# One expert's rows kept in SBUF and added by a one-hot product; earlier loads of the others; picks of three tiles on VectorE and three shifts on GpSimd

## Chip, cores, metric

One core of a Trainium2 chip runs the whole program. The metric is device time in microseconds, the median of the runs. Engines: TensorE (PE; PEld is its weight load), VectorE (DVE), ScalarE (ACT), GpSimd (POOL) and SyncE (SP, which issues most DMAs).

## The reference, cut to what matters

One encoder layer on 1152 tokens of width 1024 (1024 of a prompt, 8 x 16 of samples): a token mixer, a cross attention, and a mixture of experts, each followed by a layer norm. What the change touches is the last third:

```python
def hier_moe(x, lp):          # top-1 of 4 groups, then top-2 of 8 experts in it
    ...
    gate = (softmax(top_v) * pg[:, None]).reshape(-1)     # two gates per token
    ...
    h = silu(xb @ w_g[e]) * (xb @ w_u[e])                 # 128 rows of one expert
    return (h @ w_d[e]) * wts[:, None]
    ...
    out = zeros_like(xt).at[buf_tok].add(yb)              # two expert rows per token

x = layer_norm(ALPHA * x + hier_moe(x, lp), lp['ln3_g'], lp['ln3_b'])
```

## The kernel before

All is float32. Tokens are nine tiles of 128 rows (eight of the prompt, one of samples). The large products use two rounded parts of each operand (`high` and `low`, of type float32r) and three matmuls; products of plain float32 take two passes of TensorE for 512 columns.

*Experts.* A block is one expert with up to 128 gathered rows; there are 32 blocks (`NE`) and none more with these inputs, since no expert has over 128 rows. For block b, SyncE loads the weights (gate and up in two halves, L652, and down, L663) as VectorE frees the areas (semaphores `gu_low`, `down_low`); ScalarE rounds them (L1634, L1644), VectorE takes the remainders (`take_low`, L1747); GpSimd gathers the rows (L2357) two blocks ahead; TensorE turns them (L1292) and multiplies (L1245). The results of block b are copied from PSUM to `yo[b % 2]` by ScalarE (L1675; for the last block, in two halves, L1698 and L1700), and GpSimd scatters them to `expert_rows` in DRAM (L2364), one row for each pick: row 2 x token + k for pick k. Unused slots carry an index out of bounds and are dropped. `ye_out[u]` counts the scatters from `yo[u]`, which is also what ScalarE waits for before it fills the buffer again.

*Tail.* SyncE loads the nine tiles of x (`xl`, L689) and the layer norm's gain and shift, when the last block's gate and up products are through. Then it waits for both scatters' semaphores and loads, for each tile, the two expert rows of each token (`yk`, 1 MB a tile, L695). The weighted sum x + gate0 y0 + gate1 y1 is done for two tiles by VectorE (L2203, L2204), and for seven by TensorE: four plain float32 products with diagonal matrices of the gates (`diag`, made by VectorE in L2191; L1348) into `T[0]` or `T[1]`, which VectorE adds to x (L2199), with the row sum as a by-product. Buffers alternate, so a product waits for the sum two before it.

*Layer norm of a tile*, with p the place of the tile in the order `SEQ`: VectorE sum (`sum_rows`), its mean; ScalarE square with row sum (L1724); VectorE adds epsilon (`add_eps`, L2217); GpSimd takes the inverse root (`inverse_deviation`, L2394), on which VectorE waits for the shift factor (`shift_of`, L2212); ScalarE normalises (L1729); GpSimd multiplies by the gain (`times_gain`, L2399, both operands in SBUF); VectorE adds the shift (`add_shift`, L2222, from a copy of it in PSUM). The last two tiles are done by VectorE alone (L2227, L2232). SyncE stores tile after tile (L698). The order on each engine is written by hand. VectorE's:

```python
sum_rows(0)
for p in range(PT):                       # PT = 8
    sum_rows(p + 1)
    if p > 0: shift_of(p - 1)             # waits for root p-1 of GpSimd
    if p > 2: add_shift(p - 3)
    add_eps(p)
```

GpSimd's is: root 0; then for p from 0 to 6 the root of p+1 and the gain of p, with root 8 ahead of the last gain.

Of the kernel before, what the change touches and what calls it, by code (L numbers as in the profile page):

```python
# [49 lines left out]
def encoder_layer_kernel(nc, A, O):  # L50
# [55 lines left out]
    ye_dram = nc.dram_tensor("expert_rows", [2 * NT * P, D], f32).ap()  # L106
    ye_pairs = ye_dram.rearrange("(r k) d -> r k d", k=2)

    ctx = ExitStack()
    with ctx:  # L110
# [212 lines left out]
        yk = [area(WA + (11 + 2 * t) * D, 2, D) for t in range(NT)]  # L323
        SEQ, BY_PE = (0, 2, 1, 3, 4, 5, 6, 7, 8), (1, 3, 4, 5, 6, 7, 8)
# [101 lines left out]
        def _(sp):  # L426
# [261 lines left out]
            for t in range(NT):  # L688
                sp.dma_start(xl[t], x2_dram[t * P:(t + 1) * P, :]).then_inc(ln_in, 16)  # L689
            sp.dma_start(gain3, A["ln3_g"].to_broadcast([P, D])).then_inc(ln_in, 16)  # L690
            sp.dma_start(shift3, A["ln3_b"].to_broadcast([P, D])).then_inc(ln_in, 16)
            sp.wait_ge(ye_out[1], 16 * (NE // 2))
            sp.wait_ge(ye_out[0], 16 * more + 16 * (NE // 2))
            for t in range(NT):
                sp.dma_start(yk[t], ye_pairs[t * P:(t + 1) * P, :, :]).then_inc(last_in[t], 16)  # L695
            for n, t in enumerate(SEQ):
                sp.wait_ge(y_ready, n + 1)
                sp.dma_start(tokens(y_p, y_s, t), xl[t]).then_inc(y_out, 16)  # L698
# [3 lines left out]
            sp.wait_ge(edge_out, 16 * (4 + NB))  # L702
# [6 lines left out]
        def _(pe):  # L709
# [631 lines left out]
            for n, t in enumerate(BY_PE):  # L1341
                pe.wait_ge(last_in[t], 16)
                if n > 1:
                    pe.wait_ge(sum_done, NORMS + SEQ.index(BY_PE[n - 2]) + 1)
                out = T[n % 2]
                for k in (0, 1):
                    for c in (0, 512):
                        got = nc.tensor.matmul(out[:, c:c + 512], diag[2 * n + k], yk[t][:, k, c:c + 512], start=(k == 0), stop=(k == 1))  # L1348
                got.then_inc(picks_ps, 1)

        @block.scalar
        def _(act):
# [318 lines left out]
            def results(b, u, uses):  # L1671
                if not (isinstance(uses, int) and uses == 0):
                    act.wait_ge(ye_out[u], 16 * uses)
                act.wait_ge(down_used, 4 * b + 4)
                nc.scalar.copy(yo[u], M[1][:, :]).then_inc(ye_rows, 1)  # L1675
# [20 lines left out]
            act.wait_ge(ye_out[1], 16 * ((NE - 1) // 2))  # L1696
# [3 lines left out]
            nc.scalar.copy(yo[1][:, 512:], M[0][:, 512:]).then_inc(ye_rows, 1)  # L1700
# [14 lines left out]
            act.wait_ge(ln_in, 48 + 16 * (NT + 2))  # L1715
            act.wait_ge(ye_rows, more + NE)
            nc.scalar.copy(M[1][:, :], shift3).then_inc(gates_ready, 1)
# [20 lines left out]
        def _(dve):  # L1738
# [359 lines left out]
            nc.vector.tensor_single_scalar(route_tok[:, 0:NE], route_out[:, 0:NE], 1, ALU.logical_shift_right).then_inc(routes_ready, 1)  # L2098

# [17 lines left out]
            nc.vector.tensor_tensor(gates[:, 1, :], gates[:, 0, :], r_e2, ALU.mult)  # L2117
# [40 lines left out]
            split_down(NE - 1, (3,))  # L2158

# [28 lines left out]
            then(nc.vector.tensor_scalar(gates, gates, 1.0 / ALPHA, None, ALU.mult))  # L2188
# [4 lines left out]
            dve.wait_ge(ln_in, 48 + 16 * (NT + 2))  # L2193

            def sum_rows(p):
                u, t = p % 2, SEQ[p]
                if t in BY_PE:
                    dve.wait_ge(picks_ps, BY_PE.index(t) + 1)
                    nc.vector.scalar_tensor_tensor(xl[t], xl[t], 1.0, T[BY_PE.index(t) % 2][:, :], ALU.mult, ALU.add,  # L2199
                                                   accum_out=moments[u][:, 0:1]).then_inc(sum_done, 1)  # L2200
                else:
                    dve.wait_ge(last_in[t], 16)
                    then(nc.vector.scalar_tensor_tensor(xl[t], yk[t][:, 0, :], gates[:, 0, t:t + 1], xl[t], ALU.mult, ALU.add))  # L2203
                    nc.vector.scalar_tensor_tensor(xl[t], yk[t][:, 1, :], gates[:, 1, t:t + 1], xl[t], ALU.mult, ALU.add,  # L2204
                                                   accum_out=moments[u][:, 0:1]).then_inc(sum_done, 1)
# [27 lines left out]

            sum_rows(0)
            for p in range(PT):
# [5 lines left out]
                if p > 2:  # L2241
                    add_shift(p - 3)
                add_eps(p)

# [10 lines left out]
        def _(pool):  # L2255
# [114 lines left out]
            for b in range(NE):  # L2370
                if b + 2 < NE:
                    pool.wait_ge(xgT_ps, b + 1)
                    gather(b + 2, b % 2)
                if b > 1:
# [12 lines left out]
            pool.wait_ge(ln_in, 48 + 16 * (NT + 2))  # L2387
# [52 lines left out]
```

## Time and profile before

| | us |
|---|---|
| runs, median (lowest, highest) | 1660.57 (1656.14, 1665.41) |
| the profiled execution | 1661.41 |
| its span, first to last instruction | 1659.6 |
| mean granted TensorE clock, share of full | 0.978 |

The page gives a row of busy shares in 40 slices of 41.5 us. TensorE is near 9 tenths nearly everywhere. The experts run from about 1030 to 1607 us, with DMA at 9 tenths and 380 to 396 GB/s; the tail is the last 53 us. An average over the span says little on the tail: it has to be read from the chain of waits (what released what, back from the last instruction) and from the timeline. Times in the rows are microseconds from the start of the span.

### The profile page before, as it was taken

To read this page: it belongs to the slowest core of one execution; us is meant where nothing else is said; L and a number is where in the kernel's file an instruction comes from. 1 tells how busy PE (TensorE), PEld (TensorE's weight loads), DVE (VectorE), ACT (ScalarE), POOL (GpSimd) and SP (SyncE) were. 2 spreads that over 40 slices of the span, in tenths; PEclk is the share of its full clock that TensorE was granted. 3 is DMA by queue.
4 is the path that set the end of the run, shared out by engine and by line. 5 is a ranking of instruction groups with operands and counts; after the bars stand their busy time and mean duration, and the time that the engine had idled before them with its cause. 6 is when DMAs were issued, how large, how long until landed. Compare 5 with 4: busy or idle time off the path is not lost.

```text
span 1659.6 us, 21156 instructions
## 1 busy us (share of the span) xinstructions
PE 1585.4 (96%) x8402; PEld 1306.9 (79%) x8402; DVE 993.6 (60%) x1315; ACT 762.7 (46%) x1089; POOL 254.2 (15%) x220
## 2 busy tenths in 40 slices
PE   7999999899998999999999988999999999999966
PEld 3578887788886788999877767888888888888852
DVE  1411111477756366122455447999999898998846
ACT  2311121334436102222422222878888788888734
POOL 0000000300017471000022111111111111111105
PEclk9999999999999999999999987999999999999987
DMA  9611111510021644300335545899999999999976
GB/s 352 225 60 46 67 61 58 200 59 20 10 65 52 224 157 178 115 26 14 119 123 173 182 170 193 314 386 384 385 390 396 388 393 388 392 396 384 377 266 288
DMA packets 84001, 351.66 MB, mean 212 GB/s; under 512 B 23346, under 2 KB 26034, under 8 KB 62020
## 3 DMA queue, kind: packets, MB, share of 16 engines
q1 hardware_dynamic: 73780, 330.43, 52.7%
q0 software_dynamic: 9216, 18.89, 3.0%
q8 instruction: 64, 1.05, 0.3%
q10 hardware_dynamic: 912, 1.05, 0.2%
q14 instruction: 29, 0.24, 0.0%
HBM read 321.93 MB, written 43.15 MB: 220 GB/s over the span
## 4 chain that ended last, share of the span: by engine, by line
PE 58%; DMA 20%; DVE 13%; ACT 5%; issue 1%; SPq 1%; POOL 0%; DVEq 0%; POOLq 0%; ACTq 0%
DMA beside<-in_w_exp_up 19%; PE M L974 12%; DVE rounded L1747 11%; PE T L780 6%; PE M L771 5%; PE T L714 4%; PE M L854 4%; PE M L714 2%; ACT rounded L1634 2%; PE T L1048 2%; PE T L1046 2%; PE T L1047 2%; PE M L738 2%; PE M L1080 2%; PE M L1062 2%; PE T L1348 2%
## 5 line engine op out<-in xcount | busy, mean ns | idle before, releaser
L1747 DVE TENSOR_TENSOR rounded<-beside,rounded 128x1024 fp32r<-128x1024 f32 (+1 forms) x397 | 471.7, 1233 | 100.0 <-ACT rounded L1634 47.9
L1245 PE MATMUL M<-rounded 128*128 128x512 f32 x1920 | 467.2, 394 | 4.7 <-issue 2.5
L1245 PEld LDWEIGHTS M<-rounded 128*128 128x128 f32 x1920 | 360.3, 189 | 80.7 <-issue 2.6
L1634 ACT CAST rounded<-beside 128x1024 fp32r<-128x1024 f32 x256 | 259.3, 1050 | 79.3 <-DMA beside<-in_w_exp_up 71.9
L974 PE MATMUL M<-rounded 128*128 128x512 f32 x864 | 209.9, 398 | 2.9 <-ACT rounded L1504 1.6
L974 PEld LDWEIGHTS M<-rounded 128*128 128x128 f32 x864 | 160.6, 190 | 36.3 <-issue 2.2
L1644 ACT CAST rounded<-beside 128x1024 fp32r<-128x1024 f32 x128 | 124.9, 1048 | 27.0 <-DMA beside<-in_w_exp_down 27.0
L1747 DVE TENSOR_TENSOR rounded<-T,rounded 128x512 fp32r<-128x512 f32 (+2 forms) x98 | 92.5, 948 | 32.4 <-ACT rounded L1517 17.7
L1245 PE MATMUL T<-rounded 128*128 128x512 f32 x384 | 108.7, 398 | 0.0
L2364 POOL DMA_INDIRECT expert_rows<-beside,route_out x32 | 38.6, 1205 | 409.7 <-ACT beside L1675 389.6
L714 PE MATMUL T<-tables,arena 128*128 128x128 f32 x572 | 79.7, 283 | 15.9 <-DMA arena<-in_mem_prompt 8.0
L714 PEld LDWEIGHTS T<-tables,arena 128*128 128x128 f32 x572 | 68.2, 145 | 32.4 <-issue 9.0
L1245 PEld LDWEIGHTS T<-rounded 128*128 128x128 f32 x384 | 70.0, 189 | 13.0
L1457 ACT ACTIVATE arena<-T,negmax 128x384 f32<-128x384 f32 (+3 forms) x64 | 47.4, 740 | 71.2 <-DVE negmax L1839 71.2
L854 PEld LDWEIGHTS M<-arena 128*128 128x128 f32 x576 | 72.0, 191 | 2.6 <-DVE arena L1857 0.2
L854 PE MATMUL M<-arena 128*128 128x64 f32 x576 | 71.7, 270 | 0.1
L1046 PE MATMUL T<-rounded 128*128 128x256 f32 x248 | 71.0, 286 | 0.0
L1048 PE MATMUL T<-rounded 128*128 128x256 f32 x248 | 70.2, 283 | 0.0
L1047 PE MATMUL T<-rounded 128*128 128x256 f32 x248 | 70.2, 283 | 0.0
L780 PE MATMUL T<-rounded,x_high 128*128 128x512 f32 x270 | 65.4, 394 | 0.0
L771 PE MATMUL M<-rounded,x_high 128*128 128x416 f32 (+1 forms) x270 | 61.2, 377 | 1.4 <-ACT x_high L1368 1.1
L1899 DVE SCALAR_TENSOR_TENSOR arena<-arena,M 128x1024 f32<-128x1024 f32 x18 | 22.0, 1220 | 63.6 <-PE M L974 63.6
(339 smaller groups left out, 2345.5 us busy)
## 6 DMA issues: line engine op xcount, KB each, us to landing
beside<-in_w_exp_gate SPq DMA_DIRECT2D x64, 1024.0 KB, 7.5
beside<-in_w_exp_up SPq DMA_DIRECT2D x64, 1024.0 KB, 10.3
beside<-in_w_exp_down SPq DMA_DIRECT2D x32, 2048.0 KB, 11.7
arena<-x_rows SPq DMA_DIRECT2D x27, 512.0 KB, 4.6
x_rows<-arena SPq DMA_DIRECT2D x18, 512.0 KB, 3.0
arena<-expert_rows SPq DMA_DIRECT2D x9, 1024.0 KB, 12.7
arena<-in_x_prompt SPq DMA_DIRECT2D x16, 512.0 KB, 3.9
arena<-in_cache_mem_k SPq DMA_DIRECT2D x8, 1024.0 KB, 5.7
```

Source lines behind the costliest of these rows:

```text
L714: got = nc.tensor.transpose(out[:, k * P:(k + 1) * P] if width == P else out[0:width, k * P:(k + 1) * P], rows[:, k * width:(k + 1) * widt ...
L771: got = nc.tensor.matmul(M[u][:, at:at + c1 - c0], x[:, k * P:(k + 1) * P], part[k][:, c0:c1], start=(k == 0 and part is w_in_high and x i ...
L780: got = nc.tensor.matmul(T[u][:, c:c + CW], x[:, k * P:(k + 1) * P], part[k][:, GC + c:GC + c + CW], start=(k == 0 and part is w_in_high a ...
L854: got = nc.tensor.matmul(o, prT[n % 2][:, c, :], value[:, c, h * DV:(h + 1) * DV], start=(c == 0), stop=(c == i))
L974: got = nc.tensor.matmul(out[:, c:c + 512], x[k], part(k)[:, c:c + 512], start=(k == 0 and x is hi and part is high), stop=(k == KT - 1 an ...
L1046: nc.tensor.matmul(out, high(k)[:, d * P:(d + 1) * P], x1T[:, 0, k], start=(k == 0), stop=False)
L1047: nc.tensor.matmul(out, high(k)[:, d * P:(d + 1) * P], x1T[:, 1, k], start=False, stop=False)
L1048: got = nc.tensor.matmul(out, low(k)[:, d * P:(d + 1) * P], x1T[:, 0, k], start=False, stop=(k == KT - 1))
L1245: got = nc.tensor.matmul(out, x[xs], (high, low)[ws](w)[:, c:c + 512], start=(first and n == 0), stop=(last and n == 2))
L1634: nc.scalar.copy(as_both(high(c)), both_raw(c)).then_inc(gu_high, 1)
L1644: nc.scalar.copy(high(8 + c), down_raw[:, c, :]).then_inc(down_high, 1)
L1747: return nc.vector.tensor_tensor(out, x, highs.bitcast(f32), ALU.subtract)
```

## The change

Three things. (1) The results of the last block don't go to DRAM. ScalarE scales them by the gates of their picks while it copies them to `yo[1]` (`own_gate`, fetched with an indirect gather from the new DRAM tensor `gates_by_pick`, which SyncE writes from `gate_rows`). They are rounded and split (`y_hi`, `y_lo`), and TensorE adds them to every tile by a product with a one-hot matrix (`own_slot`, nine tiles made by VectorE from the slots' tokens). Their rows of `expert_rows` are zeroed at the start by a scatter of a cleared buffer. (2) The loads of the picked rows wait for the scatter of block 30, and for VectorE being done with the last weights, in whose areas seven of them now land. Gain and shift come behind the first two. (3) The tiles go in the order 0 to 8. VectorE does the picks of tiles 1, 4 and 7 (`sum_picks`), TensorE of the other six, and a sum of TensorE's buffer follows for all nine. GpSimd adds the shift to the first three tiles.

The diff, cut to its core:

```diff
-        SEQ, BY_PE = (0, 2, 1, 3, 4, 5, 6, 7, 8), (1, 3, 4, 5, 6, 7, 8)
+        SEQ, BY_PE = (0, 1, 2, 3, 4, 5, 6, 7, 8), (0, 2, 3, 5, 6, 8)
+        SHIFTED = 3
...
@@ SyncE, after the loads of block 1's gate and up
+                else:
+                    sp.wait_ge(kT_ready, 4 + 2 * H + 1)
+                    sp.dma_start(gates_dram.rearrange("(t p k) c -> p t (k c)", p=P, k=2), gate_rows).then_inc(edge_out, 16)
...
@@ SyncE, tail
             sp.wait_ge(gu_used, 8 * more + 8 * NE)
-            for t in range(NT):
+            for t in SEQ:
                 sp.dma_start(xl[t], x2_dram[t * P:(t + 1) * P, :]).then_inc(ln_in, 16)
-            sp.dma_start(gain3, A["ln3_g"].to_broadcast([P, D])).then_inc(ln_in, 16)
-            sp.dma_start(shift3, A["ln3_b"].to_broadcast([P, D])).then_inc(ln_in, 16)
-            sp.wait_ge(ye_out[1], 16 * (NE // 2))
+            sp.wait_ge(gu_low, 8 * more + 8 * NE)
+            sp.wait_ge(down_low, 4 * more + 4 * NE)
+            sp.wait_ge(ye_out[1], 16 + 16 * (NE // 2))
             sp.wait_ge(ye_out[0], 16 * more + 16 * (NE // 2))
-            for t in range(NT):
+            for t in SEQ:
                 sp.dma_start(yk[t], ye_pairs[t * P:(t + 1) * P, :, :]).then_inc(last_in[t], 16)
+                if t == SEQ[1]:
+                    sp.dma_start(gain3, A["ln3_g"].to_broadcast([P, D])).then_inc(mv_in, 16)
+                    sp.dma_start(shift3, A["ln3_b"].to_broadcast([P, D])).then_inc(mv_in, 16)
...
@@ TensorE, tail
+            for n, t in enumerate(SEQ):
                 if n > 1:
+                    pe.wait_ge(sum_done, NORMS + n - 1)
                 out = T[n % 2]
+                if t in BY_PE:
+                    pe.wait_ge(last_in[t], 16)
+                    for k in (0, 1):
+                        for c in (0, 512):
+                            nc.tensor.matmul(out[:, c:c + 512], diag[2 * BY_PE.index(t) + k], yk[t][:, k, c:c + 512], start=(k == 0), stop=False)
+                if n == 0:
+                    pe.wait_ge(att_high, 4 + 4 * H + 1)
+                    pe.wait_ge(kT_ready, 4 + 2 * H + 2)
+                for part in (y_hi, y_lo):
                     for c in (0, 512):
+                        got = nc.tensor.matmul(out[:, c:c + 512], own_slot[:, t * P:(t + 1) * P], part[:, c:c + 512],
+                                               start=(t not in BY_PE and part is y_hi), stop=(part is y_lo))
                 got.then_inc(picks_ps, 1)
...
@@ ScalarE, last results and tail
-            nc.scalar.copy(yo[1][:, 0:512], M[0][:, 0:512])
+            nc.scalar.activation(yo[1][:, 0:512], M[0][:, 0:512], ACT.Identity, scale=own_gate)
...
             act.wait_ge(ye_rows, more + NE)
+            nc.scalar.copy(y_hi, yo[1]).then_inc(att_high, 1)
+            act.wait_ge(mv_in, 16 * NB + 32)
             nc.scalar.copy(M[1][:, :], shift3).then_inc(gates_ready, 1)
...
@@ VectorE, before the experts; after the last splits; tail
+            then(nc.vector.tensor_scalar(gates, gates, 1.0 / ALPHA, None, ALU.mult))
+            nc.vector.tensor_copy(gate_rows, gates.rearrange("p k t -> p t k")).then_inc(kT_ready, 1)
...
+            for t in range(NT):
+                nc.vector.tensor_scalar(own_slot[:, t * P:(t + 1) * P], iota, own_token, float(-P * t), ALU.subtract, ALU.is_equal)
...
+            take_low(y_lo, yo[1], y_hi).then_inc(kT_ready, 1)
+            def sum_picks(p):
+                t = SEQ[p]
+                dve.wait_ge(last_in[t], 16)
+                then(nc.vector.scalar_tensor_tensor(xl[t], yk[t][:, 0, :], gates[:, 0, t:t + 1], xl[t], ALU.mult, ALU.add))
+                then(nc.vector.scalar_tensor_tensor(xl[t], yk[t][:, 1, :], gates[:, 1, t:t + 1], xl[t], ALU.mult, ALU.add))
...
+            sum_picks(1)
             sum_rows(0)
             for p in range(PT):
                 sum_rows(p + 1)
...
-                if p > 2:
+                if p - 3 >= SHIFTED:
                     add_shift(p - 3)
                 add_eps(p)
+                if p in (1, 4):
+                    sum_picks(p + 3)
...
@@ GpSimd, in turn 0 of the blocks, after the gather of block 2; at the end; gain of a tile
+                if b == 0:
+                    pool.wait_ge(plan_ready, 1)
+                    nc.gpsimd.memset(yo[1], 0.0).then_inc(pool_step, step.next())
...
+                    nc.gpsimd.indirect_dma_start(out=ye_dram, out_offset=bass.IndirectOffsetOnAxis(ap=route_out[:, NE - 1:NE], axis=0),
+                                                 in_=yo[1], in_offset=None, bounds_check=2 * NT * P - 1,
+                                                 oob_is_err=False).then_inc(ye_out[1], 16)
+                    pool.wait_ge(edge_out, 16 * (5 + NB))
...
+                    nc.gpsimd.indirect_dma_start(out=own_gate, out_offset=None, in_=gates_dram,
...
-            for b in (NE - 2, NE - 1):
-                scatter(b, b, b % 2)
+            scatter(NE - 2, NE - 2, 0)
...
                 nc.gpsimd.tensor_tensor(xl[t], xl[t], gain3, ALU.mult).then_inc(gain3_done, 1)
+                if p < SHIFTED:
+                    pool.wait_ge(gain3_done, p + 1)
+                    nc.gpsimd.tensor_tensor(xl[t], xl[t], shift3, ALU.add).then_inc(pads_ready, 1)
```

## Rows read from the trace of the kernel before

**Rows 1.** The page, first line.
```profile
span 1659.6 us, 21156 instructions
```

**Rows 2.** Chain of waits, 1583 to 1662: start us, us, what.
```profile
1598.98 7.33 PE M L1245 x24
...
1607.77 3.38 DMA expert_rows<-beside,route_out
...
1611.27 0.33 SPq L695
...
1611.64 6.87 DMA arena<-expert_rows
...
1618.64 26.87 PE T L1348 x56
```

**Rows 3.** Timeline, 1598 to 1612: start us, us, engine, line, operation [idle before].
```profile
1599.92 0.98 POOL L2364 DMA_INDIRECT expert_rows<-beside,route_out  x1 [14.64 <-ACT beside L1675]
...
1600.16 1.66 DVE L2191 TENSOR_SCALAR shift<-tables,gates 128x128 f32<-128x128 f32 x8
```

**Rows 4.** DMA issues in 1599-1602, 1611-1611.5, 1615-1616; last column us to landing.
```profile
expert_rows<-beside,route_out POOLq DMA_INDIRECT x1, 8.4
...
arena<-expert_rows SPq DMA_DIRECT2D x1, 1024.0 KB, 4.8
...
arena<-expert_rows SPq DMA_DIRECT2D x2, 1024.0 KB, 19.7
```

**Rows 5.** Windows: length, busy of five engines, TensorE clock, DMA share, GB/s.
```profile
1610.00:1610.50 0.50, 0.00 (x0) 0.00 (x0) 0.00 (x0) 0.50 (x1) 0.00 (x0) 0.70 0.36 147
...
1623.50:1624.00 0.50, 0.50 (x2) 0.12 (x1) 0.34 (x4) 0.15 (x1) 0.00 (x0) 0.65 1.08 459
```

**Rows 6.** Timeline of the tail; last, GpSimd's gain line (ns, min/median/max).
```profile
1616.14 1.28 DVE L2203 SCALAR_TENSOR_TENSOR arena<-arena,gates 128x1024 f32<-128x1024 f32 x1 [13.15 <-DMA arena<-expert_rows]
...
1638.47 7.03 PE L1348 MATMUL T<-arena,conv_w_rows 128*128 128x512 f32 x16
1638.67 1.22 DVE L2199 SCALAR_TENSOR_TENSOR arena<-arena,T 128x1024 f32<-128x1024 f32 x1 [0.70 <-PE T L1348]
...
1641.48 0.55 POOL L2394 TENSOR_TENSOR rstd<-moments,minus_half 128x1 f32<-128x1 f32 x1
...
1642.57 2.37 POOL L2399 TENSOR_TENSOR arena<-arena 128x1024 f32<-128x1024 f32 x1 [0.54 <-ACT arena L1729]
...
L2399 POOL TENSOR_TENSOR arena<-arena x7: 2350/2362/2368, 1628.8 to 1650.3; 128x1024 f32<-128x1024 f32 x7
```

**Rows 7.** Timeline, VectorE and GpSimd in two earlier stages, 846-855 and 560-570.
```profile
848.62 1.29 DVE L1909 SCALAR_TENSOR_TENSOR arena<-arena,moments 128x1024 f32<-128x1024 f32 x1
848.78 1.20 POOL L2267 TENSOR_SCALAR moments<-moments 128x1 f32<-128x1 f32 x1 [15.27 <-DVE moments L1905]
...
850.60 2.40 POOL L2337 TENSOR_TENSOR rounded<-beside,rounded 128x1024 fp32r<-128x1024 f32 x1
850.75 3.34 DVE L1912 SCALAR_TENSOR_TENSOR arena<-arena,rstd,shift 128x1024 f32<-128x1024 f32 x1 [0.84 <-POOL rstd L2269]
...
561.66 5.87 POOL L2314 TENSOR_TENSOR arena<-arena,conv_w_rows 128x512 f32<-128x512 f32 x3
562.92 2.20 DVE L1912 SCALAR_TENSOR_TENSOR arena<-arena,rstd 128x1024 f32<-128x1024 f32 x1
```

**Rows 8.** Around the experts' start: timeline and, first, a window (columns as rows 5).
```profile
1036.00:1040.00 4.00, 4.00 (x17) 3.21 (x17) 3.11 (x3) 3.11 (x4) 0.00 (x0) 0.90 0.00 0
...
961.06 0.95 POOL L2345 MEMSET beside<- 128x1024 f32 x1
...
1030.92 1.23 DVE L1747 TENSOR_TENSOR rounded<-T,rounded 128x1024 fp32r<-128x1024 f32 x1 [2.30 <-ACT rounded L1665]
...
1042.71 1.52 POOL L2357 DMA_INDIRECT beside<-x_rows,route_tok  x1 [11.10 <-PE T L1292]
...
1058.01 9.01 PE L1245 MATMUL M<-rounded 128*128 128x512 f32 x39
```

More of the change, by code:

```diff
@@ L322, in encoder_layer_kernel @@
         gain3, shift3 = area(WA + 9 * D, D), area(WA + 10 * D, D)
-        yk = [area(WA + (11 + 2 * t) * D, 2, D) for t in range(NT)]
-        SEQ, BY_PE = (0, 2, 1, 3, 4, 5, 6, 7, 8), (1, 3, 4, 5, 6, 7, 8)
+        yk = [area(at, 2, D) for at in (11 * D, 13 * D, 30720, 32768, 34816, 39168, 41216, 43264, 45312)]
+        SEQ, BY_PE = (0, 1, 2, 3, 4, 5, 6, 7, 8), (0, 2, 3, 5, 6, 8)
+        SHIFTED = 3
+        y_hi, y_lo, own_slot = rounded[:, 24 * D:25 * D], rounded[:, 25 * D:26 * D], rounded[:, 26 * D:26 * D + NT * P]
+        gate_rows = logits.rearrange("p t c -> p (t c)")[:, 0:2 * NT].rearrange("p (t k) -> p t k", k=2)
+        own_gate, own_token = (logits.rearrange("p t c -> p (t c)")[:, at:at + 1] for at in (2 * NT, 2 * NT + 1))
         diag = [shift2[:, i * P:(i + 1) * P] for i in range(KT)] + [conv_w[:, 2, i * P:(i + 1) * P] for i in range(4)] + [conv_w[:, 1, i * P:(i + 1) * P] for i in range(2)]
@@ L1671, in results @@
             def results(b, u, uses):
-                if not (isinstance(uses, int) and uses == 0):
-                    act.wait_ge(ye_out[u], 16 * uses)
+                if u == 1:
+                    act.wait_ge(ye_out[1], 16 * uses + 32)
+                elif not (isinstance(uses, int) and uses == 0):
+                    act.wait_ge(ye_out[0], 16 * uses)
                 act.wait_ge(down_used, 4 * b + 4)
@@ L1695, in _ @@
                     results(b - 1, 1 - u, (b - 1) // 2)
[L1696 removed]
+            act.wait_ge(ye_out[1], 16 + 16 * (NE // 2))
             act.wait_ge(down_used, 4 * NE - 2)
[L1698 removed]
+            nc.scalar.activation(yo[1][:, 0:512], M[0][:, 0:512], ACT.Identity, scale=own_gate)
             act.wait_ge(down_used, 4 * NE)
[L1700 removed]
+            nc.scalar.activation(yo[1][:, 512:], M[0][:, 512:], ACT.Identity, scale=own_gate).then_inc(ye_rows, 1)
             act.wait_ge(plan_ready, 1)
@@ L2116, in _ @@
             then(nc.vector.reciprocal(gates[:, 0, :], r_den))
-            nc.vector.tensor_tensor(gates[:, 1, :], gates[:, 0, :], r_e2, ALU.mult)
+            then(nc.vector.tensor_tensor(gates[:, 1, :], gates[:, 0, :], r_e2, ALU.mult))
+            then(nc.vector.tensor_scalar(gates, gates, 1.0 / ALPHA, None, ALU.mult))
+            nc.vector.tensor_copy(gate_rows, gates.rearrange("p k t -> p t k")).then_inc(kT_ready, 1)
             for k in (0, 1):
@@ L2185, in _ @@
                     hidden_low(b, 0)
-            then(nc.vector.tensor_scalar(gates, gates, 1.0 / ALPHA, None, ALU.mult))
             for n, t in enumerate(BY_PE):
@@ L2192, in _ @@
             got.then_inc(wukT_ready, 1)
-            dve.wait_ge(ln_in, 48 + 16 * (NT + 2))
+            dve.wait_ge(att_high, 4 + 4 * H + 1)
+            take_low(y_lo, yo[1], y_hi).then_inc(kT_ready, 1)
+            dve.wait_ge(ln_in, 48 + 16 * NT)
+            def sum_picks(p):
[3 more added lines that the diff above has]
+                then(nc.vector.scalar_tensor_tensor(xl[t], yk[t][:, 1, :], gates[:, 1, t:t + 1], xl[t], ALU.mult, ALU.add))
             def sum_rows(p):
                 u, t = p % 2, SEQ[p]
[L2197 to L2205, printed above, removed]
+                dve.wait_ge(picks_ps, p + 1)
+                nc.vector.scalar_tensor_tensor(xl[t], xl[t], 1.0, T[p % 2][:, :], ALU.mult, ALU.add,
+                                               accum_out=moments[u][:, 0:1]).then_inc(sum_done, 1)
                 dve.wait_ge(sum_done, NORMS + p + 1)
```

23 lines of the change are left out of this document (14 added, 9 removed).

## The prediction

> **What bounds the kernel now.** I read the run's own times, the page's span, then the chain of waits over the last 80 us, the timeline of that stretch engine by engine, and the DMA and clock views for what the chain leaves unexplained. The profiled execution took 1661.41 us, with a span of 1659.6 [rows 1] and 1.8 us around it; the median of the runs is 1660.57, 0.8 below it. I work out the new span, and put its difference on the median.
>
> The chain [rows 2] shows a tail of six links. The last down product ends at 1606.3, a copy follows, GpSimd issues the last scatter at 1607.77, it lands 3.38 us later, SyncE issues the loads of the picked rows at 1611.27, and TensorE then multiplies from 1618.64 without a stop for 26.87 us (56 passes) to 1645.5. From there, sum, square, normalise, gain and shifts of the last tiles and a store take 1659.6 - 1645.5 = 14.1. So the tail is the product's start, its length and 14.1. The stage before it is one in which DMA and VectorE hand the weights on, and the change leaves its weight traffic alone.
>
> **The change, part by part.**
>
> *Loads without the last scatter.* SyncE now waits for block 30's scatter, not block 31's. That one is issued at 1599.92 [rows 3] and needs 8.4 us, beside the loads of x [rows 4]: it lands at 1608.3. Two loads of gain and shift no longer stand in that stretch, so I take 1608.0 as the issue of the first load: 3.3 earlier, not the 8 that the diff suggests. Bounds: 1604 if it lands like the last one, in 3.4; 1611 if in 11. The first tile comes 4.8 after its issue, the last in 19.7 after an issue 4 later, so one each 2.45 [rows 4]. Hence tile 0 at 1612.9, tile 1 at 1615.3, gain and shift by 1617.7, tile 2 at 1620.2.
>
> *The kept rows.* The scaled copy takes the place of a copy of its size; rounding (ScalarE) and remainder (VectorE), each at most the 1.23 of a remainder of this shape [rows 8], end near 1609.4, before tile 0. Nine one-hot tiles like the twelve diagonals, eight of which take 1.66 [rows 3], fill VectorE to about 1604.7, idle there. Both are hidden by the wait for tile 0; uncovered they would be 2.5 and 1.9.
>
> *TensorE.* A picks product is 8 passes of 0.43 (16 in 7.03 [rows 6]), so 3.44 for a tile. An own product is 4 of the rounded kind, 39 of which take 9.01 [rows 8]: 0.23 each, 0.92 a tile. Before: 7 x 3.44 = 24.1. Now 6 x 3.44 + 9 x 0.92 = 28.9. The clock: 1.2 GHz from about 1610.3, 4 us after TensorE went idle, and back at 2.4 at 1623.8, 5.2 after it started [rows 5]. So tile 0's passes again start slow: 6 of 0.86, 2 of 0.43, own 0.92: from 1612.9 to 1619.9. Tile 1 (own only) 1620.8. Tile 2 waits for tile 0's sum (1621.2), then takes 4.35: 1625.6. Left alone, tiles 3 to 8 would follow to 1646.0: the start won is eaten by 4.8 us of new passes. With the 14.1 that is 1660.1, about today's.
>
> *GpSimd, where I expect the loss.* Its order is now: root of tile p+1, gain of p, and for p = 0 to 2 the shift of p too. The queue behind the shift holds the root of p+2; VectorE waits for that in the shift-factor step, with its next sums behind it, and TensorE waits for those sums to get a buffer back. A gain pass takes 2.36, a root 0.55 [rows 6]; the shift has the same shape and operands as the gain, so 2.36 too. One of the first three tiles costs 0.55 + 2 x 2.36 + 0.15 = 5.4, against TensorE's 3.3 on average. From the sum's start to the gain's it is 3.90 (1638.67 to 1642.57, [rows 6]). Tile 2's sum starts at 1625.7, which with the order of ScalarE frees tile 0's gain at 1629.6. The gain waits behind a VectorE pass (below) to 1630.3, and then: shift 0 ends 1635.1, root 2 1635.6, shift 1 1640.4, root 3 1641.0.
>
> *VectorE, picks of tiles 1, 4 and 7.* Each is two passes of 1.28 [rows 6] with both tensors in SBUF. Tile 1's lie in idle time (1615.4 to 1618). The others run beside GpSimd passes that also read SBUF. What that does is in [rows 7]: a VectorE pass of this form, 1.29 alone, takes 3.34 when a GpSimd pass of 2.40 has just begun: it waited for its end. A GpSimd operation on a single column, 1.20, ends with the VectorE pass that ran before it (849.98 and 849.91). And with both queues full they alternate: three GpSimd passes in 5.87, VectorE's second in 2.20. For tile 4 it costs GpSimd the 0.7 above. For tile 7: VectorE gets root 3 at 1641.0, wants its first pass at 1641.3, GpSimd is in gain 2 until 1643.4; the pass ends 1644.7; shift 2 goes between, to 1647.0; the second pass ends 1648.3. Sum of tile 6: 1649.5.
>
> The Trainium skill (SBUF — State Buffer, Who interferes with whom) has this as an exclusive lock, held for the whole instruction, between a VectorE instruction with two SBUF inputs and a GpSimd one that reads SBUF. By that rule the sum is the one here, without it the first rival's; the trace agrees with the rule, with 3.34 against 1.29.
>
> *The last tile.* Its product (buffer of tile 6) starts at 1649.5, and TensorE has been idle since 1641.2, 8.3 us. After 4 us idle the clock fell [rows 5], so 6 slow passes, 2 fast, own 0.9: 7.0, ending 1656.5. Plus 14.1: **1670.6**, 11.0 over 1659.6. If the clock stays, 4.4: 1654.0 and 1668.1.
>
> *Edits at or near nothing.* Moving gate scaling (0.2) ahead of the experts and adding two small copies puts some 0.6 into VectorE's queue before block 0's rows, where it idles 2.3 [rows 8]. Zeroing rows is one memset, 0.95 on this shape [rows 8], one scatter and one gather; GpSimd has nothing to do in the 11 us before 1042.7, and the DMA engines are idle from 1036 to 1040 [rows 8]. The gates go out in 1152 pieces of 8 bytes; no row prices such pieces. Behind it in GpSimd's queue is the gather of block 3, 20 us ahead of its use; behind it in SyncE's is a load whose condition comes at 1042. Bounds: a gain is excluded (nothing is taken away there), a loss up to 4 if it takes longer than these 15 us; I take 0, since the cover is known. The last scatter, gone, was on the chain and is counted above. Three adds of 1.2 leave VectorE, but early, where it waits anyway.
>
> **Rivals.**
> 1. *GpSimd is late, but the two engines don't block each other in these passes.* Then tile 7's picks end at 1643.0, its delay comes from roots 3 and 4 alone (1640.2, 1645.5), last product at 1648.8: span 1664.3, median 1665.3. Against it: [rows 7]; for it: the passes there are of other lines. Chance 0.15.
> 2. *Not slower: TensorE alone sets the end.* GpSimd takes the three shifts in its gaps; its place is the root of tiles 2 to 4, its price all of the 11.0 but 0.5. It decides if a shift pass costs under about 0.8 instead of 2.36, so that a tile's GpSimd work stays under TensorE's pace. Span 1660.1, median 1661; with the scatter of block 30 landing in 3.4 us, 4 less (1657). For it: GpSimd is idle until 1629; against it: passes of this shape all take 2.35 to 2.37. Chance 0.12, of which 0.04 for more than 0.5% faster.
> 3. *The clock doesn't fall in the gap*: 1668.1, median 1669.1. Chance 0.12.
> 4. *Later start*: the scatter of block 30 takes 11, all moves by 2.9: median 1674.5. Chance 0.08.
> 5. *The change's plumbing holds up the experts* (GpSimd sits in the wait for the gates; a gather comes late): up to 4 more, 1675.6. Chance 0.08.
> 6. The forecast, 0.45.
>
> **How the numbers follow.** 1660.57 + 11.0 = 1671.6. The range goes from 1661 (rival 2's main case) to 1677 (rivals 4 and 5 with a little over). 0.5% of this kernel is 8.3 us, about what a measurement of it can tell from no change; so slower begins at 1668.9. Above it lie nearly all of the forecast, 4, 5 and half of 3: 0.62. Within: 0.34. Faster: 0.04.
>
> **What would show it.** The first load of picked rows issued near 1608; TensorE's first picks pass near 1613, at 0.86; GpSimd's two 2.36 us passes in a row for three tiles with a root only after them; VectorE passes of the picks over 2 us for tile 7; TensorE idle some 8 us before its last product and 1.2 GHz in it. If the product runs without that gap, the forecast is wrong in its largest term (3.6 for the gap's length, 2.6 for the clock, 4.8 for passes). If the loads come at 1604, everything is 4 shorter. If the first block of the experts starts later than before, rival 5 holds.

## The result, and the profile after

The changed kernel takes 1671.14 us, median of 7 runs (1665.15 to 1675.43), against 1660.57 for the kernel before (7 runs beside it, 1656.14 to 1665.41). The ratio is 1.0054, with a 95% interval of 1.0038 to 1.0071, so it is 6.3 to 11.8 us slower. The two medians differ by 10.6; the ratio, which is not formed from them, is worth 9.0. The forecast was 1671.6.

The page of the kernel after says it only in outline. TensorE's share is still 95%; VectorE has 11 us more than before and GpSimd 13 (254.2 before).

```profile
span 1665.5 us, 21239 instructions
...
PE 1590.5 (95%) x8430; PEld 1312.2 (79%) x8430; DVE 1004.6 (60%) x1326; ACT 769.0 (46%) x1090; POOL 267.4 (16%) x225
```

The chain of waits shows where it went: start us, us, what, of the stretch from the last experts' scatter to the last product.

```profile
1596.91 7.74 DMA expert_rows<-beside,route_out
...
1604.66 4.86 DMA arena<-expert_rows
...
1609.66 5.96 PE T L1363 x8
...
1626.51 2.48 POOL arena L2446
...
1629.06 2.36 POOL arena L2449
1631.42 0.51 POOL rstd L2441
1631.93 2.35 POOL arena L2446
...
1634.36 2.36 POOL arena L2449
1636.72 0.52 POOL rstd L2441
...
1637.26 0.21 DVE shift_by L2244
...
1637.54 3.12 DVE arena L2230
...
1640.68 3.25 DVE arena L2231
...
1643.95 1.24 DVE arena L2236 x2
...
1645.24 5.25 PE T L1363 x8
1650.49 0.95 PE T L1369 x4
```

Where [rows 2] had one piece of 26.87 us of TensorE, the chain now leaves TensorE at 1623 and goes through GpSimd for 11 us: gain (L2446), shift (L2449), root (L2441), gain, shift, root. Then it goes through two VectorE passes of over 3 us (the picks of tile 7) to TensorE's last product.

The timeline of the same stretch has the three engines side by side: start us, us, engine, line, operation, and in brackets the idle time before and what ended it.

```profile
1595.97 7.33 PE L1259 MATMUL M<-rounded 128*128 128x512 f32 x24 [1.92 <-ACT rounded L1691]
...
1609.66 5.96 PE L1363 MATMUL T<-arena,shift 128*128 128x512 f32 x8 [6.36 <-DMA arena<-expert_rows]
...
1631.96 0.21 DVE L2244 TENSOR_SCALAR shift_by<-rstd,sumsq 128x1 f32<-128x1 f32 x1 [2.01 <-POOL rstd L2441]
...
1637.26 0.21 DVE L2244 TENSOR_SCALAR shift_by<-rstd,rinv 128x1 f32<-128x1 f32 x1 [2.86 <-POOL rstd L2441]
...
1637.45 3.19 DVE L2230 SCALAR_TENSOR_TENSOR arena<-arena,gates 128x1024 f32<-128x1024 f32 x1
...
1639.64 3.20 POOL L2449 TENSOR_TENSOR arena<-arena 128x1024 f32<-128x1024 f32 x1
...
1640.68 3.24 DVE L2231 SCALAR_TENSOR_TENSOR arena<-arena,gates 128x1024 f32<-128x1024 f32 x1
...
1642.80 1.53 POOL L2441 TENSOR_TENSOR rstd<-moments,minus_half 128x1 f32<-128x1 f32 x1
...
1645.24 5.25 PE L1363 MATMUL T<-arena,conv_w_rows 128*128 128x512 f32 x8 [7.01 <-DVE arena L2236]
```

VectorE waits 2.01 and 2.86 for roots that stand behind shifts. Its picks passes, 1.28 each for tile 1, take 3.19 and 3.24 for tile 7; GpSimd's shift takes 3.20 instead of 2.36 and its root 1.53 instead of 0.55. TensorE is idle 7.01 us, and its next eight passes take 5.25, where eight others take 3.70. Windows (start:end and length, busy of TensorE, weight loads, VectorE, ScalarE, GpSimd, then the granted clock, DMA share, GB/s) show the clock at its lower level, 1.2 GHz, from about 1641.6 (the window from 1641.50 has 0.57) until about 1648.4, 3.2 us into the product:

```profile
1641.00:1641.50 0.50, 0.00 (x0) 0.00 (x0) 0.50 (x1) 0.00 (x0) 0.50 (x1) 1.00 0.00 0
...
1642.00:1642.50 0.50, 0.00 (x0) 0.00 (x0) 0.50 (x1) 0.00 (x0) 0.50 (x1) 0.50 0.06 16
...
1648.00:1648.50 0.50, 0.50 (x2) 0.30 (x1) 0.50 (x2) 0.50 (x1) 0.50 (x1) 0.60 0.00 0
```

**The measure for what follows.** Some of a kernel's spread from run to run lies before the stage looked at, so I also compare *tails*: from the first pass of the last down product (the row of 24 passes) to the end of the span. Before: 1659.6 - 1598.98 = 60.6 [rows 1, 2]. After: 1665.5 - 1595.97 = 69.5, longer by 8.9. The experts' stage ahead of it, from the turn of block 0's rows to the end of the last down product, takes 577.7 before and 577.5 after. So the whole loss of the profiled execution is in the tail. The down product's 24 passes took 7.3 us in eleven of the thirteen profiled executions and 5.7 in the other two (the experiment with the all-zero operand, and the changed kernel's second). For those two it matters by 1.6 from which end of the down product one counts. The first pass is the better point, since the load that starts the tail goes out 8.7 after it both in after and in the experiment with the all-zero operand. Where an expectation speaks of the span less the end of the last down product, the figures to set it against are 53.3 before and 62.2 after.

### The profile page after: what moved, and what is told of

Its sections match the earlier page's. It is cut to its first block, busy times and chain, and to the rows that moved or that the text cites. A ratio compares the mean times of both kernels' runs of the same rounds, so it can differ in the third digit from the quotient of the medians.

```text
span 1665.5 us, 21239 instructions
## 1 busy us (share of the span) xinstructions
PE 1590.5 (95%) x8430; PEld 1312.2 (79%) x8430; DVE 1004.6 (60%) x1326; ACT 769.0 (46%) x1090; POOL 267.4 (16%) x225
## 4 chain that ended last, share of the span: by engine, by line
PE 90%; ACT 3%; DVE 3%; issue 1%; DMA 1%; POOL 1%; DVEq 0%; POOLq 0%; SPq 0%; ACTq 0%
PE M L1259 26%; PE M L988 12%; PE T L794 6%; PE M L785 5%; PE T L1259 5%; PE T L728 4%; PE M L868 4%; PE T L1306 3%; PE M L728 2%; PE T L1062 2%; PE T L1060 2%; PE T L1061 2%; PE M L1094 2%; PE M L752 2%; PE M L1076 2%; PE M L1201 1%
## 5 line engine op out<-in xcount | busy, mean ns | idle before, releaser
L1656 ACT CAST rounded<-beside 128x1024 fp32r<-128x1024 f32 x256 | 260.4, 1050 | 73.7 <-DMA beside<-in_w_exp_up 63.0
L1666 ACT CAST rounded<-beside 128x1024 fp32r<-128x1024 f32 x128 | 127.8, 1050 | 24.8 <-DMA beside<-in_w_exp_down 16.7
L2399 POOL DMA_INDIRECT expert_rows<-beside,route_out x31 | 35.7, 1152 | 342.6 <-ACT beside L1699 342.6
L868 PE MATMUL M<-arena 128*128 128x64 f32 x576 | 71.7, 270 | 0.1
L2392 POOL DMA_INDIRECT beside<-x_rows,route_tok x32 | 43.7, 1365 | 161.4 <-PE T L1306 140.4
L794 PE MATMUL T<-rounded,x_high 128*128 128x512 f32 x270 | 65.4, 394 | 0.0
L785 PE MATMUL M<-rounded,x_high 128*128 128x416 f32 (+1 forms) x270 | 61.2, 377 | 1.4 <-ACT x_high L1390 1.1
```

The costliest lines, as they stand in the source:

```text
L785: got = nc.tensor.matmul(M[u][:, at:at + c1 - c0], x[:, k * P:(k + 1) * P], part[k][:, c0:c1], start=(k == 0 and part is w_in_high and x i ...
L794: got = nc.tensor.matmul(T[u][:, c:c + CW], x[:, k * P:(k + 1) * P], part[k][:, GC + c:GC + c + CW], start=(k == 0 and part is w_in_high a ...
L868: got = nc.tensor.matmul(o, prT[n % 2][:, c, :], value[:, c, h * DV:(h + 1) * DV], start=(c == 0), stop=(c == i))
L1656: nc.scalar.copy(as_both(high(c)), both_raw(c)).then_inc(gu_high, 1)
L1666: nc.scalar.copy(high(8 + c), down_raw[:, c, :]).then_inc(down_high, 1)
```

## The experiments

**1. The shifts back on VectorE.** All else of the change stays.

```diff
-        SHIFTED = 3
+        SHIFTED = 0
```

> The changed kernel with SHIFTED = 0: GpSimd does no shift, VectorE adds it to all of the first seven tiles. I read the tail as the span less the end of the last down product: 62.2 us in the changed kernel, 53.3 in the one before. Theory 1 (a root queued behind a shift on GpSimd, the two engines blocking each other over SBUF, the clock falling in the gap): TensorE's gap before the last product shrinks from 7.8 to under 4, its clock stays, the tail falls by 7 to 8 us, to about 54.5. Theory 2 (GpSimd late, no blocking): the tail falls by 2.8, to 59.4. Theory 3 (the loss is TensorE's own products, the shifts are hidden): the tail stays within 1 us of 62.2.

Median 1662.67 beside 1661.47 of before: ratio 1.0007 (0.9997 to 1.0018), which can't be told from the kernel before. Tail 62.05, 7.45 less than after; from the end of the down product 54.7, where 54.5 was expected. (The gap that the expectation puts at 7.8 was 7.01.) Its timeline:

```profile
1600.45 7.34 PE L1259 MATMUL M<-rounded 128*128 128x512 f32 x24 [1.92 <-ACT rounded L1691]
...
1639.60 1.60 DVE L2230 SCALAR_TENSOR_TENSOR arena<-arena,gates 128x1024 f32<-128x1024 f32 x1
...
1641.24 1.28 DVE L2231 SCALAR_TENSOR_TENSOR arena<-arena,gates 128x1024 f32<-128x1024 f32 x1
...
1643.84 3.70 PE L1363 MATMUL T<-arena,conv_w_rows 128*128 128x512 f32 x8 [1.65 <-DVE arena L2236]
```

The gap is 1.65 instead of 7.01 and the last picks product 3.70 instead of 5.25: 5.36 + 1.55 = 6.9 of the 7.45. The other 0.55 lies at the start, where the scatter of block 30 landed in 6.75 instead of 7.74, which the shifts have no part in. The three shifts on GpSimd are nearly all of the loss. They took 7.9 us of GpSimd's time (2.36, 2.36 and 3.20), and some 7 reached the end.

**2. The order of GpSimd's queue or the lock?** Two edits part them. In one, the picks of tiles 4 and 7 read their addend from PSUM, so that only one tensor comes from SBUF:

```diff
-                then(nc.vector.scalar_tensor_tensor(xl[t], yk[t][:, 0, :], gates[:, 0, t:t + 1], xl[t], ALU.mult, ALU.add))
+                addend = xl[t] if p == 1 else M[1][:, :]
+                then(nc.vector.scalar_tensor_tensor(xl[t], yk[t][:, 0, :], gates[:, 0, t:t + 1], addend, ALU.mult, ALU.add))
```

(and the same in the second pass). This leaves x out of the two tiles and adds the layer norm's shift in its place, so their results are not those of the layer.

> The changed kernel, but VectorE's picks of tiles 4 and 7 read the shift's copy in PSUM as their addend in place of x in SBUF (so x is left out of these two tiles, and the shift added twice more): same passes, same order, same waits, one input in SBUF instead of two. Theory 1: tile 7's two passes take 1.28 instead of 3.2 each, the third shift of GpSimd 2.36 instead of 3.20, the gap on TensorE falls below 4.5, and the tail from 62.2 to about 56. Theory 2 (no blocking; the long passes have another cause, such as the wait on the pass before): nothing changes.

Ratio 1.0034 (1.0020 to 1.0047), tail 65.4, or 58.1 from the end of the down product where 56 was expected.

```profile
1638.45 1.27 DVE L2231 SCALAR_TENSOR_TENSOR arena<-arena,gates,M 128x1024 f32<-128x1024 f32 x1
...
1639.76 1.28 DVE L2232 SCALAR_TENSOR_TENSOR arena<-arena,gates,M 128x1024 f32<-128x1024 f32 x1
...
1640.66 2.35 POOL L2450 TENSOR_TENSOR arena<-arena 128x1024 f32<-128x1024 f32 x1
...
1642.36 5.40 PE L1363 MATMUL T<-arena,conv_w_rows 128*128 128x512 f32 x8 [3.06 <-DVE arena L2237]
...
1642.97 0.55 POOL L2442 TENSOR_TENSOR rstd<-moments,minus_half 128x1 f32<-128x1 f32 x1
```

The same instructions, in the same order, beside the same GpSimd passes: with one input in PSUM every one of the four is back at its plain duration. So the blocking is real, and hangs on VectorE's second SBUF input. It cost 69.5 - 65.4 = 4.1 us, 3.95 of it in the gap; the rest is 0.4 of an earlier start, less 0.15 in the last product. The 2.1 that I expected beyond this didn't come, and TensorE's row says why: with a gap of only 3.06 us the clock fell all the same, and the last product took 5.40.

In the other edit, the shift of tile p-1 stands after the root of tile p+1:

```diff
-                if p < SHIFTED:
-                    pool.wait_ge(gain3_done, p + 1)
-                    nc.gpsimd.tensor_tensor(xl[t], xl[t], shift3, ALU.add).then_inc(pads_ready, 1)
...
+                if 0 < p <= SHIFTED:
+                    late = SEQ[p - 1]
+                    pool.wait_ge(gain3_done, p)
+                    nc.gpsimd.tensor_tensor(xl[late], xl[late], shift3, ALU.add).then_inc(pads_ready, 1)
```

> The changed kernel, but GpSimd does each of its three shifts after the next root instead of before it; the work is the same. Theory 1: VectorE's waits for roots 2 and 3 (2.0 and 2.9 us) go, but the picks of tile 7 still meet GpSimd passes, with one more of them left: tail 2 to 3 us shorter, about 60. If only the order of the queue counted (theory 2): 5 to 6 shorter, about 57. Theory 3: no change.

Ratio 1.0049 (1.0035 to 1.0062), tail 68.3 (61.0 from the end of the down product; expected 60).

```profile
1635.47 0.21 DVE L2244 TENSOR_SCALAR shift_by<-rstd,rinv 128x1 f32<-128x1 f32 x1 [0.32 <-POOL rstd L2441]
...
1635.66 3.20 DVE L2230 SCALAR_TENSOR_TENSOR arena<-arena,gates 128x1024 f32<-128x1024 f32 x1
...
1638.90 3.25 DVE L2231 SCALAR_TENSOR_TENSOR arena<-arena,gates 128x1024 f32<-128x1024 f32 x1
...
1643.47 6.53 PE L1363 MATMUL T<-arena,conv_w_rows 128*128 128x512 f32 x8 [4.50 <-DVE arena L2236]
```

VectorE's wait for root 3 falls from 2.86 to 0.32 and the gap from 7.01 to 4.50. But the picks meet full queues as before (3.20, 3.25), the clock falls, and this time it comes back so late that the product takes 6.53. The queue's order alone is worth 2.5 us of gap, of which the slower product took 1.3 back, so 1.2 at the end. That 1.3 is not the order's: the product took 5.25 and 6.55 in two executions of the changed kernel itself (below).

**3. The clock at either end.** In the changed kernel, 28 products with an all-zero operand follow tile 7's, so that TensorE has work in its gap:

```diff
+                if n == 7:
+                    for i in range(28):
+                        got = nc.tensor.matmul(out[:, 0:512], none_slot, y_hi[:, 0:512], start=False, stop=(i == 27))
```

> The changed kernel with 28 more products on TensorE (6.6 us) behind the own product of tile 7, with an operand that is all zeros, so that nothing of the result changes: they fill the gap before the last picks product, and tile 7's buffer isn't wanted before they end. This prices the clock alone; the gap's causes stay. Theory 1: the last picks product takes 3.5 to 3.7 us instead of 5.25, the tail (62.2 in the changed kernel, span less the end of the last down product) falls by 1.6 to 60.6. If the clock has no part in the loss: no change.

Ratio 1.0043 (1.0028 to 1.0057), tail 67.9: 1.6 less than after, as expected. The gap is filled and the last picks take 3.70:

```profile
1596.30 5.70 PE L1260 MATMUL M<-rounded 128*128 128x512 f32 x24 [1.92 <-ACT rounded L1695]
...
1638.18 6.51 PE L1374 MATMUL T<-rounded 128*128 128x512 f32 x28
1645.47 3.70 PE L1364 MATMUL T<-arena,conv_w_rows 128*128 128x512 f32 x8 [0.79 <-DVE arena L2241]
```

By the measure of the expectation, from the end of the down product, nothing changed (62.2 for 62.2, not 60.6), because the down product itself took 5.70 here. That is not where the 1.6 comes from: the last picks start 49.2 after the down product's first pass here and 49.3 in after, and only then part. So of the loss, the clock's part in the last product is 1.6 in the profiled execution of after. The same at the start of the tail, with 24 products of the rounded kind ahead of tile 0's picks:

```diff
+                if n == 0:
+                    for _ in range(24):
+                        nc.tensor.matmul(T[1][:, 0:512], own_slot[:, 0:P], rounded[:, 16 * D:16 * D + 512], start=True, stop=True)
```

> The changed kernel with 24 products of no use on TensorE (into T[1], 5.6 us) between the last down product and tile 0's picks, so that the clock stays at 2.4 GHz. The first picks product takes 3.5 us instead of 6.0. Worked out from the schedule: tile 2's load lands only at about 1617 to 1618 where the last down product ends at 1603.3, so only some 1 us of the 2.5 is kept, and behind it the chain over GpSimd is as late as before: tail 61.2. If the start of TensorE's products sets the end, it is 2.5 shorter, 59.7.

Ratio 1.0049 (1.0032 to 1.0065), tail 71.7 (64.4 from the end of the down product, where 61.2 was expected): a miss.

```profile
1611.62 3.70 PE L1366 MATMUL T<-arena,shift 128*128 128x512 f32 x8 [0.57 <-DMA arena<-expert_rows]
...
1619.95 5.24 PE L1366 MATMUL T<-arena,shift 128*128 128x512 f32 x8 [2.78 <-DMA arena<-expert_rows]
```

Tile 0's picks do take 3.70 and not 5.96. TensorE is then early, and waits 2.78 for tile 2's rows, in which the clock falls again: tile 2's picks take 5.24. The slow start had been lying under the transfers. Of the 2.2 us by which this tail is longer than after's, 1.2 are there by the end of tile 2's product, and 0.9 come from the last picks, which took 6.18 for 5.25. The kernel before behaves alike, with 24 passes put ahead of its picks:

```diff
+            for _ in range(12):
+                nc.tensor.matmul(T[1][:, 0:512], ident, tables[:, 0:512], start=True, stop=True)
```

> The kernel before with twelve products of no use on TensorE (10.3 us) between the last down product and the first picks, a gap of 12.3: the clock stays at 2.4 GHz. Its first picks product took 6.3 instead of 3.4; TensorE then was never idle. By theory 1 the tail falls by what the clock cost, 2.8, less 1 for the next tile's load, which comes 4.9 after the first: from 53.3 to 51.5. If the sums on VectorE set the pace: no change.

Ratio 0.9993 (0.9982 to 1.0005), tail 60.3, 0.3 less instead of the 1.8 expected. Its timeline:

```profile
1605.40 10.46 PE L1342 MATMUL T<-tables 128*128 128x512 f32 x24
1618.59 15.70 PE L1350 MATMUL T<-arena,shift 128*128 128x512 f32 x32 [2.73 <-DMA arena<-expert_rows]
```

The added passes end 2.73 before the first picked rows come. TensorE starts at the full clock, and then the clock falls 0.5 us into the product (the window from 1619.00 shows 0.62, those from 1619.5 to 1622.5 show 0.50): most of the slow stretch is only moved. The 56 passes are 0.9 shorter, and start 0.7 later after the down product's first pass than before, which leaves the 0.3.

**4. What is left without the shifts.** Experiment 1 has the early loads, and is still 1.4 behind the kernel before in its tail. The next three start from it. In the first, the picked rows are loaded only after the remainder of the kept rows is out:

```diff
+            sp.wait_ge(kT_ready, 4 + 2 * H + 2)
             for t in SEQ:
                 sp.dma_start(yk[t],
```

> The changed kernel without GpSimd's shifts, the loads of the picked rows held back until VectorE has split the kept rows, which comes 3.4 us after the end of the last down product where the first load went out 0.4 to 1.4 after it. This prices the early start. Theory 1: each microsecond later is one at the end: the tail, from the first pass of the last down product, goes from 62.1 to 64 to 65 (2 to 3 later). If TensorE's or VectorE's work hides the start: 62.1.

Ratio 1.0020 (1.0008 to 1.0033), tail 65.2, 3.2 more than experiment 1 (64 to 65 was expected). SyncE's rows of the first load, experiment 1 and then this one:

```profile
1608.16 0.80 SPq L703 DMA_DIRECT2D arena<-expert_rows  x2
```

```profile
1609.48 0.80 SPq L704 DMA_DIRECT2D arena<-expert_rows  x2
```

Counted from the start of the last down product that is 7.71 and 10.80 (1609.48 - 1598.68). Loads 3.1 later end 3.2 later: an early load is worth its full length, and the step the change rests on works. In the kernel before the same figure is 1611.27 - 1598.98 = 12.3, so experiment 1 wins 4.6 there and gives 6.0 back. Is it the new passes on TensorE? The next kernel does only the high part of each own product and leaves the remainder of the kept rows out of the result, 18 passes less:

```diff
-                for part in (y_hi, y_lo):
+                for part in (y_hi,):
```

> The changed kernel without GpSimd's shifts (as in the first experiment), and the own product only with the rounded part of the kept rows, its remainder left out: 2 passes a tile instead of 4, so 18 of 0.23 us fewer, 4.1 us. I now read the tail from the first pass of the last down product to the end of the span: 60.6 before, 69.5 changed, 62.1 without GpSimd's shifts. If TensorE's own products are what is left of the loss (1.4): the tail falls by 1 to 2, to about 60.6 (not by 4.1: VectorE's passes are nearly as tight there). If they are covered: 62.1.

Ratio 1.0006 (0.9995 to 1.0018), tail 62.3 where 60.6 was expected: a miss.

```profile
1641.45 5.16 PE L1363 MATMUL T<-arena,conv_w_rows 128*128 128x512 f32 x8 [3.04 <-DVE arena L2236]
```

The passes taken away left a gap of 3.04 where experiment 1 had 1.65. VectorE sets the pace by then: its picks of tile 7, 2.06 (beside a GpSimd pass) and 1.28, stand ahead of the sum that frees the buffer. The last picks start 0.8 earlier, the own product behind them is half a microsecond shorter, and the clock's fall took 1.46 back. The last of the three takes tile 7's picks off VectorE and gives them to TensorE:

```diff
-        SEQ, BY_PE = (0, 1, 2, 3, 4, 5, 6, 7, 8), (0, 2, 3, 5, 6, 8)
+        SEQ, BY_PE = (0, 1, 2, 3, 4, 5, 6, 7, 8), (0, 2, 3, 5, 6, 7, 8)
...
-                if p in (1, 4):
+                if p == 1:
```

> The kept rows and the early loads nearly alone: the changed kernel without GpSimd's shifts, and with tile 7's picks on TensorE again (seven tiles there as before, two on VectorE). TensorE has 7 x 3.44 + 9 x 0.92 = 32.4 us of passes against 24.1 before, from a start some 9 us earlier in the run's own clock than the one before (6.4 instead of 12.3 after the last down product). If TensorE sets the end: its last product ends at 6.4 + 2.5 (slow clock) + 32.4 + 0.5 = 41.8 after the last down product, and 14.1 more gives a tail of 55.9, against 54.7 measured without GpSimd's shifts and 53.3 before. If VectorE's picks for tile 7 were the dearer place for them, the tail is under 54.7.

Ratio 1.0022 (1.0013 to 1.0032), tail 63.8 (56.5 from the end of the down product; expected 55.9). From tile 2 on TensorE runs to the end with no gap over half a microsecond, here into its last picks,

```profile
1644.46 3.59 PE L1363 MATMUL T<-arena,conv_w_rows 128*128 128x512 f32 x8
```

and the tail is 1.7 longer than in experiment 1, 0.3 of it from a later start. So picks on VectorE do pay, by some 1.5 of the 3.6 us that they take from TensorE.

**5. A version made of what helped.** No shifts on GpSimd, tile 7's picks one tile earlier on VectorE, gain and shift loaded after the third tile, and the 24 products at the start:

```diff
-        SHIFTED = 3
+        SHIFTED = 0
...
-                if t == SEQ[1]:
+                if t == SEQ[2]:
...
-                if p in (1, 4):
-                    sum_picks(p + 3)
+                if p in (1, 3):
+                    sum_picks(4 if p == 1 else 7)
```

> A version meant to be the best of the changed kernel: no shifts on GpSimd, picks of tile 7 on VectorE one tile earlier (after the step that waits for the sum of tile 4), gain and shift loaded behind tile 2 instead of tile 1, and 24 products of no use to keep TensorE's clock up until tile 0 is there. In the run with these products alone TensorE waited 2.8 us for tile 2's load and lost the clock there; that load comes 2.4 earlier now. Theory 1: TensorE's first gap is filled, its second gone, tail 52 (54.7 without GpSimd's shifts alone, 53.3 before): as fast as the kernel before or 1 to 2 us faster. If the start is worth nothing: 54 to 55.

Ratio 1.0001 (0.9989 to 1.0014), tail 60.1 to the 60.6 of before; from the end of the down product 52.8, where 52 was expected. It can't be told from the kernel before.

**6. The changed kernel once more.**

> The changed kernel once more, beside the two others on the same chip: is its tail, 69.5 from the first pass of the last down product, the same in another execution, and its ratio to the kernel before again 1.005? The schedule of the tail hangs on few waits, so I expect 69 to 70, whatever the time of the stages before it. Outside of 68 to 71, the readings of the single profiles above would be less sure.

Ratio 1.0050 (1.0033 to 1.0066), tail 70.1, just above the 69 to 70 expected, with the same gap:

```profile
1650.04 6.55 PE L1363 MATMUL T<-arena,conv_w_rows 128*128 128x512 f32 x8 [7.03 <-DVE arena L2236]
```

The gap repeats to 0.02 us. The time at which the clock comes back doesn't: 6.55 for the product behind it, 5.25 the first time. The two tails of one kernel differ by 0.6, so less than that between two single tails here (0.3 in the kernel before with 24 passes more, 0.5 in experiment 5, 0.3 between the kernel with the high part only and experiment 1) says nothing.

## Why the prediction was right

The main step held: a short root behind a long shift in GpSimd's queue, then VectorE's picks blocked against GpSimd, then a gap in TensorE, and slow passes after it. Counted from the end of the last down product (1606.3 in the prediction, 1603.3 in after), step by step:

| | predicted | measured |
|---|---|---|
| first load of picked rows issued | 1.7 | 1.4 |
| tile 0's picks start | 6.6 | 6.4 |
| tile 0's product ends | 13.6 | 13.3 |
| tile 2's product ends | 19.3 | 19.3 |
| gain 0 starts | 24.0 | 23.2 |
| root 2 done | 29.3 | 28.6 |
| root 3 done | 34.7 | 33.9 |
| picks of tile 7 done | 42.0 | 40.6 |
| last product starts | 43.2 | 41.9 |
| last product ends | 50.2 | 48.1 |
| end of span | 64.3 | 62.2 |

- **The start.** The scatter of block 30 took 7.74 beside the loads of x, where [rows 4] had 8.4, and 6.75 to 7.75 in the experiments that keep this order of loads. The load starts 3.6 earlier than before, for the 3.3 I took. Experiment 4 shows that this gain is real and one for one.
- **TensorE.** 0.94 for an own product (predicted 0.92), 3.6 to 3.7 for picks at the full clock (3.44). Tile 0's product took 6.9 for 7.0.
- **GpSimd.** 2.36 for a shift, as the gain line said. A round of gain, shift and root took 5.3 for 5.4. Gain 0 came 0.8 sooner, since the delay that I gave it from tile 4's picks was not there: they were all but over, at 1626.73, when it started at 1626.51.
- **The blocking.** Two picks passes took 6.5, for the 7.0 I gave them. Experiment 2 turns this from an argument into a shown cause, at 4.1 us. The Trainium skill (SBUF — State Buffer, Who interferes with whom) gives the rule, and by it a version with one input in PSUM should be free of it; the passes of 1.27 and 1.28 agree.
- **Two terms were too big:** the gap, 8.3 for 7.0, and the last product, 7.0 for 6.2 (7.5 in the second profiled execution, so that one has no single value). Together they are the 2.1 by which the tail was shorter than the sum. The gap came out too long because gain 0 was put 0.8 too late and the blocked passes 0.5 too long.
- **The median** came out at +10.6, where the ratio on record says +9.0 and the tails +8.9 and +9.5. The forecast of +11.0 is nearer to the median than its terms deserve: that it came within 0.5 us of it is in part luck. The stretch ahead of the experts differs between executions by far more than this (block 0's turn starts at 1025.8 in the first profiled execution of the changed kernel and at 1032.9 in the second). The interval of 6.3 to 11.8 holds all of these figures.
- **A sum that doesn't close.** For TensorE left alone the prediction's own terms bring tiles 3 to 8 from 1625.6 to 1644.9, not 1646.0: 1.1 us of it have no term. The forecast doesn't rest on it, but rival 2's time does.
- **The end**: 14.04 from the last sum for 14.1.

**The rivals.** No blocking (1): experiment 2 is its test, and shows the blocking. Its time of 1664.3 doesn't follow from its last product at 1648.8 either: with 4.4 for that product and 14.1 behind it, it would be 1667.3. TensorE alone (2): would need a shift pass under 0.8; it took 2.36. Take the shifts away and about its time comes (experiment 1, 1.2 over before, for 0.5), but not by its path alone: the load goes out 1.3 earlier than forecast, and a gap of 1.65 before the last picks is still there. The clock stays up (3): it fell. A later start (4): the load came at 1.4, not 4.6. The plumbing (5): GpSimd had all of it behind it at 1039.86, as its timeline shows,

```profile
1032.26 0.95 POOL L2411 MEMSET beside<- 128x1024 f32 x1 [3.59 <-DVE plan L2169]
1034.11 1.56 POOL L2414 DMA_INDIRECT expert_rows<-beside,route_out  x1 [0.89 <-POOL beside L2411]
1038.35 1.51 POOL L2419 DMA_INDIRECT logits<-gates_by_pick,route_out  x1 [2.69 <-DMA gates_by_pick<-logits]
1040.17 1.07 POOL L2392 DMA_INDIRECT beside<-x_rows,route_tok  x1 [0.31 <-issue]
```

and the gather of block 3 was out at 1040.2. The 1152 pieces of 8 bytes cost one wait of 2.69 in a stretch where GpSimd had 11 us to spare [rows 8]. The experts' stage was 0.2 shorter than before. The zero that I took for it was right.

**The balance of the change.** Early loads give 3.6 to 4.6. The own products (9 x 0.94 = 8.5 us, for 3.7 of picks taken off TensorE) and VectorE's work take about 6.0, a part of which can't be had back by cutting passes (experiment 4). GpSimd's shifts take 7.45 more: 4.1 through the blocking, and 3.3 through the order of the queue and what is behind it. That split goes by taking the blocking away first; the two and the clock overlap, and the 7.45 and the 4.1 hold 0.5 and 0.4 of an earlier start. The 6.0 is what is left over in the sum; no experiment measures it by itself. With experiment 1 in the middle the sum closes: -4.6 + 6.0 + 7.45 = 8.9.

## What to carry to other kernels

A long pass handed to an engine because it is idle costs what stands behind it in that engine's queue. Look for the short step (here a root on one column) for which another engine waits, and add the pass's length to it. Keep a VectorE pass with two SBUF inputs out of a stretch in which GpSimd's queue is full, or read one of the two from PSUM. And before speeding up the start of a stage, or cutting passes in it, look at what is late next: here TensorE once only reached the next load sooner, and once lost to the clock what the cut had given.

## What the runs showed of the hardware

- **Short gaps.** Ahead of the change the clock had been seen to fall some 4 us after TensorE went idle [rows 5]. It fell 3.3 after in the first profiled execution of after (idle from 1638.2, fallen by about 1641.6), and can fall sooner still, as windows of the kernel with the high part only show (columns as above), TensorE idle from 1638.4 to 1641.45:

```profile
1640.50:1641.00 0.50, 0.00 (x0) 0.00 (x0) 0.50 (x1) 0.00 (x0) 0.50 (x1) 1.00 0.00 0
1641.00:1641.50 0.50, 0.05 (x1) 0.05 (x1) 0.47 (x4) 0.00 (x0) 0.50 (x1) 0.51 0.00 0
```

  It was at 1.2 GHz 2.6 us after the last pass. With gaps of 3.06 (experiment 2, one input in PSUM) and 2.73 (the kernel before with 24 passes more) it fell only when TensorE had begun again, 0.8 and 0.5 us into its passes; with one of 1.65 it stayed up. The price for the eight passes behind such a gap was 1.5 to 2.9 us (5.16 to 6.55 instead of 3.70), and differed between executions of the same kernel.
- **A fall that comes or not.** After the same idle 1.92 ahead of the last down product, its 24 passes took 7.33 in the first profiled execution of after and 5.73 in the second. The windows of the first show 0.50 from 1597.5 to 1600.5, those of the second 1.00 throughout.
- **Full queues alternate.** Two VectorE passes of 1.28 among GpSimd passes of 2.36 took 6.5, and a GpSimd root of 0.55 took 1.53: in these rows each engine waits for one instruction of the other every time, not for the queue to run dry.
